# Four transformer layers on one core: stage ends and beginnings by token block, five weight slots with the low half in place

## The chip, the cores and the metric

The kernel runs on one core of one Trainium2 chip. The metric is the device time of the program in microseconds (us). Inputs and output are float32 in HBM.

## The reference

256 tokens of width 1024 pass through four layers. Layers 0 and 1 are RMS-normalised, layers 2 and 3 use LayerNorm:

```python
# layers 0, 1: MLA mixer, then dilated mixer (DIL)
h = h + rms_norm(mixer(rms_norm(h, g[0])), g[1])
h = h + rms_norm(swiglu(rms_norm(h, g[2]), ffn_w_in[i], ffn_w_out[i]), g[3])
h = h + (p[i] @ ple_w_proj[i]) * sigmoid(h @ ple_w_gate[i])
# layers 2, 3: retention, block attention and convolution side by side
h = layer_norm(alpha * h + mix(h) @ w_out)
h = layer_norm(alpha * h + (gelu(conv(h @ up_left)) * (h @ up_right)) @ w_down)
```

The hidden width of every FFN is 2816. All weights are used once, so the program is a stream of 251 weight chunks of up to 1 MB.

## The kernel before, in words

The five engines run five hand-written programs, synchronised by semaphores. The tokens form two blocks of 128 (`TB` = 2, called block 0 and block 1, `tb` in the code).

**The weight stream.** Each chunk c (128 x 2048 floats at most) takes slot c % 3. SP issues its DMA into `raw` (`stream`, line 358) once POOL has split chunk c - 3 (`lo_split`). ACT rounds it to `w_hi` (`hi_part`, line 917) once the DMA has landed and PE has used chunk c - 3 (`chunk_used`), and POOL writes the rest, `raw - w_hi`, to `w_lo` (`lo_part`, line 403). `ahead(c)` on ACT stands wherever chunk c is worked on and splits chunk c + 2. Every product is three matmuls (hi x hi, hi x lo, lo x hi; line 423).

**Two forms of product.** In a wide chunk (wo, FFN out, gate, proj, and the first chunks of layers 2 and 3) the tokens are the stationary operand and 512 columns of weights move: `wide_block` is 12 matmuls for one token block. In a tile chunk (FFN in, DIL's q and k) 128 columns of weights are stationary and the 256 tokens move: `tiles_product` is 48 matmuls for both blocks at once.

**Stage ends and beginnings.** `wide_end` takes the last two chunks of wo (of DIL, layers 2 and 3) and of FFN out for block 0, signals `y0_ready`, then takes them for block 1. DVE then makes each block's new h (`add_rms_y`, a norm by scalar Newton steps at lines 1331 and 1337, ending at line 1398; `layer_norm`, ending at line 1484), PE turns it by eight transposes (`turn_block`, line 530), ACT copies the turned tiles to `xt_hi` (lines 932 and 934), DVE writes `xt_lo` (lines 1410 and 1414), and PE begins the next stage. `begin` takes two wide chunks for block 0 and then for block 1 (gates, layers 2 and 3). An FFN or DIL begins with both blocks turned. In layers 0 and 1 the row scale of the next norm comes later: ACT squares h, DVE makes `rstd` (`rms_r`), PE spreads it (`turn_r`), and DVE multiplies the products by it.

**FFN.** Tile chunk u writes PSUM bank u % 3 of three; PE waits for `hidden_ready` of tile u - 3. DVE and ACT make the hidden tile in `conv` and `gate`. PE, ACT, POOL, SP and DVE run these stages in hardware loops (`Fori`).

**PLE.** `ple` does the gate and projection chunks whole; ACT takes both sigmoids after the last gate chunk; DVE multiplies, adds and hands h to the next stage. The split p (`p_hi`, `p_lo`) is made at the start.

## Time and profile before

| | us |
|---|---|
| median of three runs | 1620.15 (1620.07 to 1621.26) |
| the profiled execution, its own time | 1619.89 |
| its span, first to last instruction | 1618.1 |
| PE busy with matmuls | 1494.7 (92%) |
| POOL busy | 1060.0 (66%) |
| DVE busy | 840.3 (52%) |
| ACT busy | 756.2 (47%) |
| mean granted PE clock | 0.965 of full speed |

A line of the timeline reads: start, duration, engine, line of the kernel, operation, output and inputs, shape, count; in brackets the idle time of the engine before it and who ended it. Matmuls overlap in the record, so a matmul's cost is the distance between starts, not its duration. "PE psum L530 <- DVE h L1484" means that PE's instruction at line 530 waited for DVE's at line 1484.

### The profile page before, as it was taken

Reading aid. Unit: us, or ns where it says so; the run is one execution under the profiler, and the core shown is the slowest. Engines: PE = TensorE matmul, PEld = TensorE weight load, DVE = VectorE, ACT = ScalarE, POOL = GpSimd, SP = SyncE. Lnnn points to the kernel's source line nnn. Section 1 sums busy time; section 2 is a strip of 40 time slices with the busy share of each in tenths; the row PEclk is TensorE's granted clock in tenths of the full one; section 3 lists DMA queues with packets and bytes.
Section 4 is the critical chain, followed back from the end, with each engine's and each line's share of the span. In section 5 each row is a group of like instructions: output and inputs, shape, how many; then the busy total and the mean of one; then the engine's idle time right before and its main releaser. Section 6 shows DMA issues by size and latency. Waiting matters only on the chain.

```text
span 1618.1 us, 26225 instructions
## 1 busy us (share of the span) xinstructions
PE 1494.7 (92%) x10190; PEld 1372.1 (85%) x10190; DVE 840.3 (52%) x1269; ACT 756.2 (47%) x856; POOL 1060.0 (66%) x255
## 2 busy tenths in 40 slices
PE   6897999998999999989999999779999797799996
PEld 5786999878999999789987789679998697599985
DVE  5546888024222322388841254567860458568833
ACT  6774554344544444555543445235543344255531
POOL 4254788865665555568887586358888575378883
PEclk9997999999999999989999999879999899799999
DMA  5383555545555555345555555335565555245551
GB/s 208 98 293 123 182 181 182 182 156 180 174 184 162 167 171 172 130 144 181 181 182 182 183 189 182 104 105 182 181 208 182 168 172 175 78 148 183 182 214 53
DMA packets 63346, 271.15 MB, mean 168 GB/s; under 512 B 5978, under 2 KB 28688, under 8 KB 36273
## 3 DMA queue, kind: packets, MB, share of 16 engines
q1 hardware_dynamic: 38300, 242.62, 44.3%
q10 hardware_dynamic: 24981, 27.61, 5.1%
q8 instruction: 48, 0.79, 0.2%
q14 instruction: 17, 0.14, 0.0%
HBM read 269.08 MB, written 8.21 MB: 171 GB/s over the span
## 4 chain that ended last, share of the span: by engine, by line
PE 83%; DVE 11%; ACT 4%; issue 1%; POOL 1%; DMA 0%; ACTq 0%; SPq 0%; DVEq 0%
PE psum L423 81%; DVE rstd L1337 2%; DVE newton L1331 1%; PE psum L740 1%; PE psum L530 1%; ACT w_hi L917 1%; ACT xt_hi L932 1%; DVE psum L1480 1%; DVE cv L1692 1%; DVE psum L1470 1%; POOL w_lo L403 1%; DVE h L1484 1%; DVE cv L1688 0%; DVE var L1716 0%; DVE xt_lo L1410 0%
## 5 line engine op out<-in xcount | busy, mean ns | idle before, releaser
L403 POOL TENSOR_TENSOR w_lo<-raw,w_hi 128x2048 fp32r<-128x2048 f32 (+3 forms) x251 | 1059.8, 4228 | 535.5 <-ACT w_hi L917 535.2
L917 ACT ACTIVATE w_hi<-raw 128x2048 fp32r<-128x2048 f32 (+3 forms) x251 | 450.2, 1794 | 515.9 <-PE psum L423 497.0
L423 PE MATMUL psum<-xt_hi,w_hi 128*128 128x256 f32 x1984 | 569.6, 287 | 7.1 <-DVE xt_lo L1410 5.8
L423 PE MATMUL psum<-xt_hi,w_lo 128*128 128x256 f32 x1984 | 565.9, 285 | 0.0
L423 PE MATMUL psum<-xt_lo,w_hi 128*128 128x256 f32 x1984 | 565.9, 285 | 0.0
L423 PEld LDWEIGHTS psum<-xt_hi,w_hi 128*128 128x128 f32 x1984 | 385.7, 194 | 14.8 <-issue 14.7
L423 PEld LDWEIGHTS psum<-xt_lo,w_hi 128*128 128x128 f32 x1984 | 385.7, 194 | 0.1
L423 PEld LDWEIGHTS psum<-xt_hi,w_lo 128*128 128x128 f32 x1984 | 385.3, 194 | 0.0
L423 PE MATMUL psum<-w_hi,xt_hi 128*128 128x384 f32 (+3 forms) x408 | 143.3, 364 | 15.7 <-DVE xt_lo L1414 9.5
L1443 DVE TENSOR_TENSOR conv<-conv,gate 128x256 f32<-128x256 f32 x44 | 144.8, 3292 | 1.5
L423 PE MATMUL psum<-w_hi,xt_lo 128*128 128x384 f32 (+3 forms) x408 | 140.2, 357 | 0.0
L423 PE MATMUL psum<-w_lo,xt_hi 128*128 128x384 f32 (+3 forms) x408 | 140.1, 356 | 0.0
L1446 DVE CAST ht_hi<-conv 128x256 f32 x88 | 120.6, 1371 | 12.3 <-DVE conv L1443 2.1
L423 PE MATMUL psum<-w_lo,ht_hi 128*128 128x512 f32 x352 | 111.0, 396 | 0.0
L423 PE MATMUL psum<-w_hi,ht_lo 128*128 128x512 f32 x352 | 111.0, 396 | 0.0
L423 PE MATMUL psum<-w_hi,ht_hi 128*128 128x512 f32 x352 | 111.0, 396 | 0.0
L423 PEld LDWEIGHTS psum<-w_hi,xt_hi 128*128 128x128 f32 x408 | 77.8, 191 | 26.5 <-issue 11.8
L423 PEld LDWEIGHTS psum<-w_hi,xt_lo 128*128 128x128 f32 x408 | 77.9, 191 | 7.3
L423 PEld LDWEIGHTS psum<-w_lo,xt_hi 128*128 128x128 f32 x408 | 78.0, 191 | 7.0
L423 PEld LDWEIGHTS psum<-w_hi,ht_lo 128*128 128x128 f32 x352 | 66.3, 188 | 16.2
L423 PEld LDWEIGHTS psum<-w_lo,ht_hi 128*128 128x128 f32 x352 | 66.3, 188 | 16.2
L423 PEld LDWEIGHTS psum<-w_hi,ht_hi 128*128 128x128 f32 x352 | 66.0, 188 | 15.8
(214 smaller groups left out, 1484.5 us busy)
## 6 DMA issues: line engine op xcount, KB each, us to landing
raw<-w_tail SPq DMA_DIRECT2D x156, 1024.0 KB, 4.9
raw<-w_dil SPq DMA_DIRECT2D x24, 1024.0 KB, 4.8
raw<-w_mix SPq DMA_DIRECT2D x24, 1024.0 KB, 4.8
raw<-w_dil SPq DMA_DIRECT2D x16, 576.0 KB, 4.0
bias_tiles<-bias_rows ACTq DMA_DIRECT2D x1, 6912.0 KB
gbuf<-gain_rows ACTq DMA_DIRECT2D x12, 512.0 KB, 5.4
dbias<-bias_tiles ACTq DMA_DIRECT2D x16, 384.0 KB, 4.9
raw<-w_mla_a SPq DMA_DIRECT2D x3, 1024.0 KB, 7.9
```

Of the source, the lines that this page charges most:

```text
L403: nc.gpsimd.tensor_tensor(w_lo[:, s, 0:width], raw[:, s, 0:width], w_hi[:, s, 0:width].bitcast(F32), ALU.subtract).then_inc(lo_split, 1)
L423: return nc.tensor.matmul(dst, lhsT, rhs, start=start, stop=stop)
L530: ins = nc.tensor.transpose(psum[:, bank, n * P:(n + 1) * P], src[:, tb, kt * P:(kt + 1) * P], ident[:, :])
L740: ins = nc.tensor.transpose(flat[:, 5 * BANK + j * P:5 * BANK + (j + 1) * P], prob1[:, j * P:(j + 1) * P], ident[:, :])
L917: nc.scalar.activation(w_hi[:, s, 0:width], raw[:, s, 0:width], ACT.Copy).then_inc(hi_split, 1)
L932: ins = nc.scalar.activation(dst[:, kt, tok], src, ACT.Copy, scale=table_of(gains, GAINED, t, kt))
L1331: ins = v.scalar_tensor_tensor(w, y, y, half, ALU.mult, ALU.mult)
L1337: ins = v.scalar_tensor_tensor(y, w, 1.5, y, ALU.add, ALU.mult)
L1443: step(v.tensor_tensor(hid, hid, gate[:, u % SLOTS, :], ALU.mult))
L1446: step(v.tensor_copy(hi, hid))
L1470: step(v.scalar_tensor_tensor(rows, h[:, tb, :], ALPHA, rows, ALU.mult, ALU.add))
L1480: step(v.scalar_tensor_tensor(rows, rows, mv[:, tb, 0:1], gbuf[:, 0, :], ALU.subtract, ALU.mult))
```

## The change

- **Five slots, low half in place.** `raw` and `w_lo` become the same memory: POOL writes `w_lo` over `raw`. SP's DMA of chunk c waits until PE has used chunk c - 5; ACT waits only for the landing. `ahead(c)` splits chunk c + 3. ACT's copies in MLA have the true widths (1152, 512, 512 instead of 2048, 2048, 512).
- **Three last chunks by block.** `wide_end` holds three chunks: block 0 of all three, `y0_ready`, then block 1. Block 0's transposes for the next stage stand before block 1 of the last chunk (layers 0 and 1), or midway in it (layers 2 and 3). MLA and DIL end in the same way, with single blocks of wo put between the last attention steps.
- **First chunks by block.** An FFN of layers 0 and 1 and DIL begin with two tile chunks, an FFN of layers 2 and 3 with three, for block 0, then the turn of block 1, then the same chunks for block 1. `tile_part` moves 128 tokens instead of 256. Gates 2 and 3 and proj are taken by block too, with a sigmoid and an addition for each block.
- **Around it.** DVE writes `xt_lo` of block 0 before it starts block 1's norm. p is split late in each FFN, into `ot_hi` and `ot_lo`. `conv`, `gate` and `cv` share one buffer. The loops of PE, ACT, POOL and SP are written out; DVE keeps its loops.

```diff
-SLOTS = 3
+SLOTS = 5
+GROUP = 6
+LEAD = 3
+HOLD = 3
+LANES = 3
...
-        raw = sb("raw", [P, SLOTS, W])
+        with ExitStack() as part:
+            raw = sb("raw", [P, SLOTS, W], F32, part)
+        w_lo = sb("w_lo", [P, SLOTS, W], F32R)
...
-                    sp.wait_ge(lo_split, c - SLOTS + 1 + per * i)
+                    sp.wait_ge(chunk_used, c - SLOTS + 1)
...
+            def begin(t, cs, cols, part):
+                views = []
+                for k, c in enumerate(cs):
+                    views.append(chunk(c, cols))
+                    part(k, *views[k], 0)
+                turn_block(t, 1)
+                for k, view in enumerate(views):
+                    part(k, *view, 1).then_inc(chunk_used, 1)
+
+            def tile_part(t, bank0):
+                def part(k, hi, lo, tb):
+                    tok = slice(tb * P, (tb + 1) * P)
+                    for half in range(2):
+                        f = slice(half * P, (half + 1) * P)
+                        dst = psum[:, bank0 + k, half * SEQ + tb * P:half * SEQ + (tb + 1) * P]
+                        for kt in range(KT):
+                            arrive(t, tb, kt)
+                            ins = split_w(dst, hi[:, kt, f], lo[:, kt, f], xt_hi[:, kt, tok], xt_lo[:, kt, tok],
+                                          kt == 0, kt == KT - 1)
+                    return ins
+                return part
...
+            def wide_end(c, n, lhs, at, then, late, down=False, ready=lambda k: None):
+                first = n - HOLD
+                views = []
+                for k in range(HOLD):
+                    views.append(chunk(c + first + k, D))
+                    ready(k)
+                    ins = wide_block(0, first + k, *views[k], n, lhs, at, down)
                 ins.then_inc(y0_ready, 1)
+                for k, view in enumerate(views):
+                    if k == HOLD - 1 and then is not None:
+                        turn_early = lambda: turn_block(then, 0)
+                        if not late:
+                            turn_early()
+                        ins = wide_block(1, first + k, *view, n, lhs, at, down, turn_early if late else None)
+                    else:
+                        ins = wide_block(1, first + k, *view, n, lhs, at, down)
+                    ins.then_inc(chunk_used, 1)
...
+                held = 2 if l < 2 else LANES
+                begin(t, [C_IN[l] + u for u in range(held)], 2 * P, tile_part(t, FFN_AT[l]))
...
+                begin(t, (C_GATE[l], C_GATE[l] + 1), D, gate_part)
+                gates = [chunk(C_GATE[l] + m, D) for m in (2, 3)]
+                for m in (2, 3):
+                    ins = wide_block(0, m, *gates[m - 2], PROJ_N, xt, gate_at)
+                ins.then_inc(gate0_ready, 1)
+                pe.wait_ge(p_ready, l + 1)
+                proj = chunk(C_PROJ[l], D)
+                wide_block(0, 0, *proj, 1, ot, proj_at).then_inc(y0_ready, 1)
+                for m in (2, 3):
+                    wide_block(1, m, *gates[m - 2], PROJ_N, xt, gate_at).then_inc(chunk_used, 1)
+                turn_block(then, 0)
+                wide_block(1, 0, *proj, 1, ot, proj_at).then_inc(chunk_used, 1)
...
+            begin(T_DIL, (C_DIL, C_DIL + 1), 2 * P, tile_part(T_DIL, 0))
             turn_r(3, T_DIL)
+            d_tiles(2, 0)
...
-                act.wait_ge(landed[s], 16 * (c // SLOTS + 1) + 16 * turns)
-                if c >= SLOTS:
-                    act.wait_ge(chunk_used, c - SLOTS + 1 + more)
-                width = HI_WIDTHS[c]
+                act.wait_ge(landed[s], 16 * (c // SLOTS + 1))
+                width = WIDTHS[c]
...
-                if c + 2 < CHUNKS:
-                    hi_part(c + 2, more, turns)
+                if c + LEAD < CHUNKS:
+                    hi_part(c + LEAD)
...
+            def border(t, y, c, normed):
                 for tb in range(TB):
+                    if y is not None:
+                        y_squares(y, tb)
+                    if tb == 1:
+                        ahead(c)
                     turn_hi_block(t, xt_hi, tb)
+                    if normed:
+                        act.wait_ge(rows_ready, rows_of(t) + tb + 1)
+                        h_squares(tb)
```

What moves on PE at the end of FFN 0 (`ht` is the hidden tile, `h` the block to be turned, `xt` the turned h for the gates). Before, the first transposes follow the last matmul of block 1:

```order
L423 MATMUL psum<-w_hi,ht_hi 128x512 x2
L423 MATMUL psum<-w_lo,ht_hi 128x512 x2
L423 MATMUL psum<-w_hi,ht_lo 128x512 x2
L530 MATMUL psum<-ident,h 128x128 [waits rows_ready]
L530 MATMUL psum<-ident,h 128x128 x7
L423 MATMUL psum<-w_hi,xt_hi 128x512 [waits xt_ready,lo_split]
```

Now the last chunk's block 1 stands behind them:

```order
L409 MATMUL psum<-w_hi,ht_lo 128x512 x2
L535 MATMUL psum<-ident,h 128x128 [waits rows_ready]
L535 MATMUL psum<-ident,h 128x128 x7
L409 MATMUL psum<-w_hi,ht_hi 128x512 x2
L409 MATMUL psum<-w_lo,ht_hi 128x512 x2
L409 MATMUL psum<-w_hi,ht_lo 128x512 x2
L409 MATMUL psum<-w_hi,ht_hi 128x512 x2
L409 MATMUL psum<-w_lo,ht_hi 128x512 x2
L409 MATMUL psum<-w_hi,ht_lo 128x512 x2
L409 MATMUL psum<-w_hi,xt_hi 128x512 [waits xt_ready,lo_split]
```

So twelve matmuls lie between the turn of block 0 and the first gate matmul that needs it. On ACT at the same place (`gate` and `conv` are the squares' unused outputs, called `lanes` in the change), before:

```order
L944 ACTIVATE gate,stat<-psum 128x512 [waits y0_ready]
L944 ACTIVATE gate,stat<-psum 128x512 [waits y_gained]
L917 ACTIVATE w_hi<-raw 128x2048 [waits chunk_used,landed2]
L944 ACTIVATE conv,stat<-psum 128x512 [waits chunk_used]
L944 ACTIVATE conv,stat<-psum 128x512 [waits y_gained]
L934 ACTIVATE xt_hi<-psum 128x4x128 [waits turned] x4
```

and now:

```order
L960 ACTIVATE lanes,stat<-psum 128x512 [waits y0_ready]
L960 ACTIVATE lanes,stat<-psum 128x512 [waits y_gained]
L954 ACTIVATE xt_hi<-psum 128x4x128 [waits turned] x2
L960 ACTIVATE lanes,stat<-psum 128x512 [waits chunk_used]
L960 ACTIVATE lanes,stat<-psum 128x512 [waits y_gained]
L937 ACTIVATE w_hi<-raw 128x2048 [waits landed4]
L954 ACTIVATE xt_hi<-psum 128x4x128 [waits turned] x2
```

The split of the next weight chunk has moved from between the two blocks' squares to right behind block 1's, and it waits for its landing only. At the start of FFN 0 on PE, the matmuls that moved 256 tokens move 128:

```order
L409 MATMUL psum<-xt_hi,w_lo 128x128
L409 MATMUL psum<-xt_hi,w_hi 128x128
L409 MATMUL psum<-xt_lo,w_hi 128x128
L409 MATMUL psum<-xt_hi,w_lo 128x128
L535 MATMUL psum<-ident,h 128x128 [waits rows_ready]
L535 MATMUL psum<-ident,h 128x128 x7
L409 MATMUL psum<-xt_hi,w_hi 128x128 [waits xt_ready]
```

Between block 0 and block 1 of the two chunks stands only block 1's turn.

## Rows read from the trace of the kernel before

**Rows 1.** PE's waits over the whole span: total us, times, longest
```profile
PE psum L530 <- DVE h L1484: 28.9, 5, 6.2
...
PE psum L530 <- DVE h L1398: 11.7, 4, 5.5
PE psum L423 <- DVE xt_lo L1414: 10.8, 6, 3.4
PE psum L423 <- DVE xt_lo L1410: 7.9, 4, 2.5
...
PE psum L423 <- ACT probT L1091: 3.4, 3, 1.1
```

**Rows 2.** PE's timeline at the borders B0, B2, B3 and B5
```profile
129.75 1.22 PE L423 MATMUL psum<-w_hi,ot_hi 128*128 128x512 f32 x2 [2.22 <-DVE ot_lo L1573]
...
147.48 0.55 PE L423 MATMUL psum<-xt_hi,w_hi 128*128 128x256 f32 x1 [1.63 <-DVE xt_lo L1410]
...
155.95 0.60 PE L423 MATMUL psum<-ident,rstd 128*128 128x128 f32 x4
...
374.15 1.09 PE L530 MATMUL psum<-ident,h 128*128 128x128 f32 x8 [1.56 <-DVE h L1463]
...
671.62 0.66 PE L423 MATMUL psum<-ident,rinv_q 128*64 128x128 f32 x8 [1.22 <-ACT probT L1176]
...
691.77 1.97 PE L530 MATMUL psum<-ident,h 128*128 128x128 f32 x8 [5.51 <-DVE h L1398]
...
935.62 0.50 PE L423 MATMUL psum<-w_hi,xt_hi 128*128 128x512 f32 x1 [0.61 <-POOL w_lo L403]
```

**Rows 3.** PE's timeline in the first chunks: 22, 44 and 23 matmuls between starts
```profile
19.95 0.40 PE L423 MATMUL psum<-w_lo,xt_hi 128*128 128x512 f32 x1
...
24.96 0.39 PE L423 MATMUL psum<-w_hi,xt_lo 128*128 128x512 f32 x1
...
25.48 0.28 PE L423 MATMUL psum<-w_hi,xt_hi 128*128 128x160 f32 x1
...
30.40 0.28 PE L423 MATMUL psum<-w_hi,xt_lo 128*128 128x160 f32 x1
...
42.44 0.28 PE L423 MATMUL psum<-w_hi,xt_hi 128*128 128x256 f32 x1
...
45.18 0.28 PE L423 MATMUL psum<-w_hi,xt_lo 128*128 128x256 f32 x1
```

**Rows 4.** All engines, block 1 of B0: RMS norm on DVE, ACT beside it
```profile
139.06 0.68 DVE L1387 TENSOR_TENSOR t<-psum,gbuf 128x512 f32<-128x512 f32 x1
...
140.37 2.16 ACT L932 ACTIVATE xt_hi<-psum,gains 128x128 fp32r<-128x128 f32 x8
...
142.54 1.28 DVE L1398 SCALAR_TENSOR_TENSOR h<-t,rstd,h 128x1024 f32<-128x1024 f32 x1
```

**Rows 5.** DVE at the end of the program: block 0's LayerNorm begins, then block 1's
```profile
1600.32 1.23 DVE L1470 SCALAR_TENSOR_TENSOR psum<-h,psum 128x1024 f32<-128x1024 f32 x1 [48.94 <-PE psum L423]
...
1607.77 1.22 DVE L1470 SCALAR_TENSOR_TENSOR psum<-h,psum 128x1024 f32<-128x1024 f32 x1
```

**Rows 6.** All engines in block 0's LayerNorm at B7
```profile
1048.41 1.92 ACT L917 ACTIVATE w_hi<-raw 128x2048 fp32r<-128x2048 f32 x1 [6.24 <-PE psum L423]
...
1050.41 4.50 POOL L403 TENSOR_TENSOR w_lo<-raw,w_hi 128x2048 fp32r<-128x2048 f32 x1 [3.57 <-ACT w_hi L917]
1050.55 4.37 DVE L1337 SCALAR_TENSOR_TENSOR rstd<-newton,rstd 128x1 f32<-128x1 f32 x1
...
1055.21 0.16 DVE L1337 SCALAR_TENSOR_TENSOR rstd<-newton,rstd 128x1 f32<-128x1 f32 x1
```

**Rows 7.** The page's DMA issues: size, median us from issue to landing
```profile
raw<-w_tail SPq DMA_DIRECT2D x156, 1024.0 KB, 4.9
```

**Rows 8.** ACT in the third step of MLA
```profile
80.64 1.92 ACT L917 ACTIVATE w_hi<-raw 128x2048 fp32r<-128x2048 f32 x1
...
88.05 0.62 ACT L917 ACTIVATE w_hi<-raw 128x512 fp32r<-128x512 f32 x1
```

More of the change, by code:

```diff
@@ L895, in _ @@
                 t = (T_RET2, T_RET3)[n]
-                turn(t, t1, block_ready(t))
+                for tb in range(TB):
+                    turn_block(t, tb, t1)
                 pe.wait_ge(cv_copied, 3 * n + 3)
@@ L960, in turn_hi_rms, with squares, h_squares, y_squares @@
-            def turn_hi_rms(t):
-                for tb in range(TB):
+            def squares(tb, src, col, n=D, at=0):
+                return nc.scalar.activation(unused[tb][:, at:at + src.shape[-1]], src, ACT.Square, scale=n ** -0.5,
+                                            accum_out=stat[:, col:col + 1])
+            def h_squares(tb):
+                squares(tb, h[:, tb, :], 2 * TB + tb).then_inc(h_squared, 1)
+            def y_squares(y, tb):
+                if tb == 0:
+                    act.wait_ge(y0_ready, YS.index(y) + 1)
+                else:
+                    act.wait_ge(chunk_used, y_chunk(*y) + 1)
+                rows = y_rows(y, tb)
+                squares(tb, rows[:, 0:BANK], 2 * tb).then_inc(squared, 1)
+                act.wait_ge(y_gained, TB * RMS_YS.index(y) + tb + 1)
+                squares(tb, rows[:, BANK:], 2 * tb + 1, at=BANK).then_inc(squared, 1)
@@ L1042, in _, with mla_heads @@
                                      accum_out=stat[:, TB + tb:TB + tb + 1]).then_inc(squared, 1)
-            turn_hi(T_MLA_C, xt_hi)
+            for tb in range(TB):
+                turn_hi_block(T_MLA_C, xt_hi, tb)
             gq, gk = MLA_GROUP * MLA_HD, MLA_GROUP * NOPE
-            def mla_heads(at, more=0, turns=0, between=None, after=None):
+            def mla_heads(at, between=None, after=None):
                 c = C_MLA + 3 * at
-                ahead(c, more, turns)
+                ahead(c)
                 if between is not None:
                     between()
-                act.wait_ge(chunk_used, c + 1 + more)
+                act.wait_ge(chunk_used, c + 1)
                 for tb in range(TB):
@@ L1070, in mla_heads @@
                     after()
-                ahead(c + 1, more, turns)
+                ahead(c + 1)
             def mla_qT(step):
@@ L1597, in _ @@
             add_rms_y(("out", 0), 1, 1, T_PLE0)
[L1598 to L1601 removed]
+            ple(0, T_DIL)
             rms_r()
```

521 lines of the change are left out of this document (221 added, 300 removed).

## The prediction

> **What bounds the kernel now.** I read the waits of TensorE (PE) first, then PE's timeline at the ends of the stages, then what the vector engine (DVE), the scalar engine (ACT) and POOL do there. Inside the FFN and DIL stages PE has no gap; its gaps lie where one stage hands a normalised h to the next. [Rows 1] sum them: 28.9 and 11.7 us for h of a token block, 10.8 and 7.9 for the low half xt_lo of the turned h, DVE the releaser every time. [Rows 2] show single ones. After a long gap PE runs at its lower clock (1.2 instead of 2.4 GHz): the 48 matmuls of the first chunk of FFN 0 lie between 147.48 and 155.95, 8.5 us, where they take 5.7 at full clock, and eight transposes at 691.77 take 1.97 instead of the 1.09 at 374.15. Call the borders B0 (wo to FFN 0), B1 and B4 (FFN to the gate of layers 0 and 1), B2 (layer 0 to DIL), B3 (to FFN 1), B5 (layer 1 to layer 2), B7 and B10 (wo to FFN 2 and 3), B8 (layer 2 to 3), and the end.
>
> **The price of working by token block.** From [rows 3], starts divided by the matmuls between them: 160 columns 4.92/44 = 0.112 us, 256 columns 2.74/23 = 0.119, 512 columns 5.01/22 = 0.228. From 256 to 512 columns the step is about 0.107 us, so the moving data go at 0.42 ns a column; at that slope 160 columns should take 0.079. They take 0.112: a floor that isn't the moving data. Weights (w) of 128 columns stand in front of every one of these matmuls, and I take this floor for 128 columns too. The bounds are 0.066 (the slope alone) and 0.112. The value is the upper one, since 160 is the nearest row and already lies on the floor. The Trainium skill (TensorE: Matmul & The Clock Gate, on LDWEIGHTS) gives the load of a weight as its columns over 1.2, 107 ns for 128: by that rule the row agrees. The same page's sustained roofline says about 81 ns a matmul at N=128, which would make the extra 24.7 us instead of 59.8; it stands beside rival (b).
>
> The wide chunks (wo, out, gate, proj, mix) hold the tokens as weights and move 512 columns of w, so they split by block for nothing: 12 matmuls, 2.7 us a block. A tile chunk (FFN in, DIL) moves the tokens. Split, its 48 matmuls of 256 columns become 96 of 128: 96 x 0.1115 = 10.7 us for 48 x 0.119 = 5.7, **5.0 us more a chunk**. Two chunks at B0, B2, B3 and three at B7, B10 are 12 chunks: **+59.8 us** of PE time that was not there.
>
> **What the tile borders give back.** Before, gaps and half clock [rows 1, 2], the slow matmuls estimated as in the first chunk of FFN 0: B0 2.2+2.2+3.3+1.6 and some 5.5 slow, 14.8; B2 1.6+2.5 and 1.7 slow, 5.8; B3 5.5+1.6, two waits of 1.2 in the last DIL pair and 3.2 slow, 12.8; B7 12.1 (6.2, 5.2 and 0.7; it and B10 hold 22.8 of the 28.9) and about 4.3 slow, 16.4, B10 the same. Together 66.2.
> New gaps: PE now has 10.7 or 16 us of work on block 0 while DVE makes block 1's h, but still waits for its own transposes: 1.9 us each time where gains are applied in four steps (half the transposes, ACT's four steps of 0.29, DVE's the same), 1.0 elsewhere. B0 2 x 1.9; B2 1.9, and 1.4 because the third chunk takes the first one's bank and so waits for turn_r, rb_dil and the first dqk (before, a chunk lay between); B3 2 x 1.9 plus 1.4 (exponentials of the last pair behind only one 2.7 us block) and 1.9 (o_scaled, ot_hi, ot_lo with nothing between values_sum and wo's last chunk); B7 and B10 0.6 and 1.0. Together 17.4. Net of the five borders: 59.8 - 66.2 + 17.4 = **+11.0 us**.
>
> **The other borders.** One norm takes DVE 4.8 us in RMS form [rows 4] and 7.45 in LayerNorm form [rows 5].
> B1 and B4: block 0 is ready 0.3 us after PE asks, Z (the last chunk) then covers its turn, and the gates' block 0 gives 5.4 us of cover to block 1's norm of 4.8. That would be 1.2 us better than before. But ACT's order puts the split of the next chunk right behind the second square of block 1. In [rows 4] ACT's next instruction begins 1.31 us after DVE's first (T), a split takes 1.92 and POOL follows 0.08 later, at T+3.31; h begins at T+3.48. [Rows 6] show what then happens: POOL begins 0.1 us before an rstd that takes 0.16 elsewhere, and the rstd takes 4.37, to the end of POOL's 4.50. So I take h1 at T+9.1 instead of T+4.8; PE waits 3.7 us, turns and begins block 1 at half clock: **+5 us each**, bounds -1.2 and +7. The Trainium skill (SBUF — State Buffer, on the shared port pair) has it that a DVE operation with two SBUF inputs and a GpSimd one that reads SBUF exclude each other for a whole instruction; the rows agree. At B0 and B3 the same collision comes, but the 10.7 us of block 0 hide it.
> B5: **-2.2** (a gap of 2.3 goes, of the 10.8, and the wait of 0.6 for w_lo [rows 2]; 1.0 comes). B8: before 6.1+3.4+0.2 of gaps and 2.9 slow; now 0.3 for block 0, 2.9 for block 1 (7.45 plus 0.9 behind POOL, against 5.5 of cover), 0.9 for the turn and 1.5 slow: **-7.0**. The end: three blocks instead of two lie between y0_ready and the last matmul, 8.4 us, longer than block 0's 7.45, so block 1's norm begins right at the last matmul instead of 2.0 us later: **-2.0**.
>
> **The rest.** The slots: a chunk's DMA now starts when the chunk five before is used; it takes 4.9 us [rows 7], the split 1.9, POOL 4.5, 11.4 together against four chunks of 5.5 or more. No wait, if that holds. MLA: ACT splits 512 columns where it split 2048, 0.6 for 1.9 us [rows 8], ahead of probT, in two of the three steps where PE waits 3.4 us in all for it [rows 1]: **-2.2** (0 to -3.4). Start: the third split now precedes the squares; the Newton steps move 2 us into POOL's three operations: **+1.5** (0 to +3). PE's loops written out: FFN's matmuls are 0.001 us apart wider than straight ones, 72 chunks: **-2** (0 to -4.7). The p split moves to ACT and DVE inside FFN, where both wait for PE: 0; if not, a DVE operation of 0.7 us ahead of a border.
>
> **Sum.** 11.0 + 10 - 2.2 - 7.0 - 2.0 - 2.2 + 1.5 - 2 = +7.1. The profiled execution's time is 1619.9 (span 1618.1; 0.3 below the median of 1620.15): the profiled one would come to 1627.0, and the difference to the median lies inside every other uncertainty here: **1627**.
>
> **Rivals.**
> (a) POOL comes late at B1 and B4: the margin is 0.17 us. If POOL begins 0.2 us later than I reckon, h goes first. 2 x 6.2 less: 1614.6, **faster**. For it: both ends move with every semaphore; against: in [rows 6] POOL was in just that place. Chance 0.2.
> (b) 128 columns cost less than the floor of 160, because the next weights load partly behind the matmul: say 0.085 us, between the bounds. Then 1152 x 0.0265 = 30 less, some 8 of it returned as waits for h1 at B0 and B3: 1605. Against it are the matmuls of 160 columns, same types, 48 in a row. Chance 0.05. With the skill's 81 ns (the page above) it would be 35 less instead of 30.
> (c) The covers are worth more than I count: all gaps of more than 2 us go, the clock stays up, and my new gaps (17.4 us, each by handovers of 0.05 to 0.1) are a third too large, 5.8 less: 1621, no change. Chance 0.22.
> (d) Refill too late: SP's request waits for PE and no longer for POOL, and near the borders three chunks are held. If a landing takes 10 us there, two waits of 2 to 4 us come at each of four borders: +15, 1640. Against it: 4.9 us at 1 MB, and five slots. Chance 0.06.
> My forecast has 0.47.
>
> **The numbers.** A measurement of this kernel tells from no change what is over 0.2%, 3.2 us. Slower: forecast 0.47 less its lower edge, and (d): 0.5. Same: (c) and part of the forecast's edge: 0.22. Faster: (a), (b) and the low side of (c): 0.28. The range reaches from 1608, inside (a) with its bounds, to 1635, B1 and B4 at +7 with start and MLA at their worse ends; the forecast's own is 1620 to 1634.
>
> **What would show it.** Matmuls xt,w of 128 columns: 1152, starts 0.11 us apart. At B1 and B4 an h of 5 to 6 us instead of 1.3 with POOL beside it. B7's gaps gone but the stretch from Z to the fourth chunk no shorter. DVE's last operation 2 us nearer to PE's last. I am wrong if the 128-column matmuls lie under 0.09 us apart, if h at B1 takes 1.3 us, or if PE waits for POOL's w_lo inside stages.

## The result, and the profile after

The changed kernel takes **1732.05 us** (median of 4 runs, 1727.69 to 1733.49), the one before 1620.33 in the same session: ratio **1.0684, 95% interval 1.0663 to 1.0705**. The forecast was 1627, range 1608 to 1635. The direction was right and the size was not: 7 us more were expected, and 112 came. The direction is not owed to the causes that were missed: with both of them removed (below) the changed kernel still takes 1639.46. The profiled execution took 1730.88, with a span of 1729.1.

PE is busy for 93% of the span, so the lost time is not in long gaps. The waits of PE over the whole span, total, times, longest (against [rows 1]):

```profile
PE psum L409 <- DVE ht_lo L1458: 31.4, 26, 1.7
PE psum L535 <- DVE t L1729: 17.5, 2, 8.8
PE psum L409 <- DVE xt_lo L1421: 10.9, 6, 2.0
PE psum L535 <- DVE h L1409: 8.2, 3, 3.6
...
PE psum L409 <- DVE xt_lo L1425: 6.9, 6, 1.5
PE psum L857 <- ACT mvr L1272: 4.8, 2, 2.6
PE psum L535 <- DVE h L1497: 4.3, 4, 2.8
```

What the change was made for happened: the waits for h of a LayerNorm fell from 28.9 to 4.3 us. But at the top is a wait that [rows 1] do not have: for ht_lo, the last thing that DVE makes of an FFN tile. Busy time by stretch, for PE, PEld (PE's weight loads), DVE, ACT and POOL, with the number of instructions, then the granted clock of TensorE (1.00 is full), the share and the GB/s of the DMA; first the kernel after, then the one before:

```profile
150.00:200.00 50.00, 46.96 (x272) 46.36 (x272) 27.23 (x46) 15.39 (x21) 19.49 (x5) 0.66 0.29 95
200.00:250.00 50.00, 46.02 (x378) 45.21 (x377) 44.22 (x40) 17.50 (x15) 36.46 (x9) 1.00 0.48 163
...
426.00:446.00 20.00, 20.00 (x97) 20.00 (x97) 7.71 (x23) 3.53 (x5) 7.03 (x3) 0.51 0.33 92
...
1154.00:1189.00 35.00, 34.02 (x303) 33.78 (x302) 18.41 (x30) 11.00 (x10) 17.43 (x4) 1.00 0.28 92
1550.00:1600.00 50.00, 50.00 (x419) 50.00 (x418) 40.60 (x53) 20.70 (x18) 40.67 (x9) 1.00 0.53 181
```
```profile
150.00:200.00 50.00, 50.00 (x406) 50.00 (x406) 39.55 (x46) 26.40 (x23) 38.05 (x9) 0.97 0.45 152
200.00:250.00 50.00, 50.00 (x419) 50.00 (x419) 41.57 (x42) 27.61 (x23) 40.53 (x9) 1.00 0.53 184
```

There are two separate losses. At the starts of FFN 0 (150 to 200), DIL (426 to 446) and FFN 1 PE is busy nearly all the time at a clock of 0.51 to 0.66 (FFN 1: 0.56 from 750 to 800). And inside FFN 0, at full clock, PE does 378 matmuls in 50 us instead of 419, and POOL is busy for 36.46 us instead of 40.53. FFN 3, at 1550, is as fast as before.

**The clock.** PE at the start of FFN 0, in DIL's second block, after it at the end of FFN 0's split, and at FFN 2 (start, duration):

```profile
138.91 0.28 PE L409 MATMUL psum<-xt_hi,w_hi 128*128 128x128 f32 x1
...
139.36 0.28 PE L409 MATMUL psum<-xt_lo,w_hi 128*128 128x128 f32 x1
139.47 0.37 PE L409 MATMUL psum<-xt_hi,w_lo 128*128 128x128 f32 x1
139.64 0.41 PE L409 MATMUL psum<-xt_hi,w_hi 128*128 128x128 f32 x1
```
```profile
425.73 0.33 PE L409 MATMUL psum<-xt_hi,w_hi 128*128 128x128 f32 x1 [1.95 <-DVE xt_lo L1421]
...
426.43 0.42 PE L409 MATMUL psum<-xt_hi,w_lo 128*128 128x128 f32 x1
426.64 0.41 PE L409 MATMUL psum<-xt_hi,w_hi 128*128 128x128 f32 x1
```
```profile
183.59 0.41 PE L409 MATMUL psum<-xt_hi,w_lo 128*128 128x256 f32 x1
183.80 0.32 PE L409 MATMUL psum<-xt_hi,w_hi 128*128 128x256 f32 x1
183.96 0.28 PE L409 MATMUL psum<-xt_lo,w_hi 128*128 128x256 f32 x1
```
```profile
1154.22 0.28 PE L409 MATMUL psum<-xt_lo,w_hi 128*128 128x128 f32 x1
1154.33 0.27 PE L409 MATMUL psum<-xt_hi,w_lo 128*128 128x128 f32 x1
```

The starts lie 0.11 us apart at first, as forecast. Then, 1.3 us into running matmuls at 139.47 and 0.5 us into them at 426.23, the distance becomes 0.213: half clock (1.2 GHz). In both places PE had waited 2.0 us for xt_lo just before. (A wait of that length does not always do it: in the run with the products in PSUM, below, the first block of FFN 0 ran at 0.112 throughout behind a wait of 2.05 us, and the second, behind 1.96, at 0.214.) The distance stays there for 84 and 95 matmuls at FFN 0, 90 in DIL, 85 and 95 at FFN 1, and rises at 183.80, 1.4 us after the first 256-column matmuls. At FFN 2 and 3, where the waits ahead of the two blocks are 0.6 (for h) and 1.0 us (for xt_lo), all 288 keep 0.112. In the kernel before, where 256-column matmuls began at 147.48 [rows 2], the granted clock was full again at 153.5. The Trainium skill (TensorE: Matmul & The Clock Gate, The HAM clock gate) has it that the slow state is the default "and activity releases the throttle". The rows of DIL do not agree: PE is busy for 20.00 of 20.00 us at a granted clock of 0.51, and the measurement decides. The 449 slow matmuls (84 + 95 + 90 + 85 + 95) at 0.101 us more each are **45 us**.

**The FFN tile.** DVE in FFN 0, one tile and the cast of the next; then POOL, of which the first row is two operations; then ACT:

```profile
238.61 3.55 DVE L1454 TENSOR_TENSOR lanes<-lanes 128x256 f32<-128x256 f32 x1
242.29 4.48 DVE L1457 CAST ht_hi<-lanes 128x256 f32 x1
246.90 0.43 DVE L1458 TENSOR_TENSOR ht_lo<-lanes,ht_hi 128x256 f32 x1
...
249.17 0.29 DVE L1457 CAST ht_hi<-lanes 128x256 f32 x1
```
```profile
237.25 9.38 POOL L401 TENSOR_TENSOR w_lo<-raw,w_hi 128x2048 fp32r<-128x2048 f32 x2 [3.37 <-ACT w_hi L937]
249.99 4.63 POOL L401 TENSOR_TENSOR w_lo<-raw,w_hi 128x2048 fp32r<-128x2048 f32 x1 [3.37 <-ACT w_hi L937]
```
```profile
247.69 0.42 ACT L1001 ACTIVATE lanes<-lanes 128x256 f32<-128x256 f32 x1 [7.27 <-DVE lanes L1438]
248.01 1.90 ACT L937 ACTIVATE w_hi<-raw 128x2048 fp32r<-128x2048 f32 x1
```

Before the change (DVE, then POOL, FFN 0):

```profile
206.07 3.49 DVE L1443 TENSOR_TENSOR conv<-conv,gate 128x256 f32<-128x256 f32 x1
209.70 0.29 DVE L1446 CAST ht_hi<-conv 128x256 f32 x1
210.12 0.43 DVE L1447 TENSOR_TENSOR ht_lo<-conv,ht_hi 128x256 f32 x1
```
```profile
204.65 4.62 POOL L403 TENSOR_TENSOR w_lo<-raw,w_hi 128x2048 fp32r<-128x2048 f32 x1 [1.13 <-ACT w_hi L917]
210.41 4.62 POOL L403 TENSOR_TENSOR w_lo<-raw,w_hi 128x2048 fp32r<-128x2048 f32 x1 [1.14 <-ACT w_hi L917]
```

Before, in FFN 0 and 1, each tile met one POOL operation: DVE's multiply waited for its end at 209.27, and cast and subtraction just fitted into the 1.14 us in which POOL rested. After, POOL does two chunks one behind the other (9.38 us); the multiply waits for the first (3.55) and the cast for the second (4.48). ACT's gate stands 7.27 us behind DVE, its next split behind the gate, and POOL then idles 3.37 us with two chunks to come. This cycle of two tiles takes 9.38 + 3.37 = 12.75 us, where PE needs 11.5, and it repeats: PE's waits for ht_lo come 12.8 us apart, 9 each in FFN 0 and 1, and 8 in FFN 2, there 13.5 apart. The 256-column matmuls of the hidden stages: 960 each in 127.8 us in FFN 0 and 1, 912 in 124.0 in FFN 2 and in 109.6 in FFN 3. At FFN 3's 0.1201 us 960 take 115.3, so the loss is 12.5 + 12.5 + 14.4 = **39 us**. One collision a tile costs PE nothing: in FFN 2 and 3 of the kernel before, every cast is held by POOL already (2.0 to 2.9 us where 0.29 is needed), and PE has no wait for ht_lo; FFN 3 after the change is the same (1.8 to 3.7 us).

**What the forecast had right** stands in the same trace. The collision at B1 (DVE, then POOL):

```profile
377.58 0.16 DVE L1353 SCALAR_TENSOR_TENSOR rstd<-newton,rstd 128x1 f32<-128x1 f32 x1
377.77 5.46 DVE L1409 SCALAR_TENSOR_TENSOR h<-t,rstd,h 128x1024 f32<-128x1024 f32 x1
```
```profile
377.58 4.57 POOL L401 TENSOR_TENSOR w_lo<-raw,w_hi 128x2048 fp32r<-128x2048 f32 x1 [9.71 <-ACT w_hi L937]
```

POOL began 0.19 us ahead of h (reckoned: 0.17), h took 5.46 instead of 1.3, and PE waited 3.56 (reckoned: 3.7).

### The profile page after: what moved, and what is told of

Read it like the earlier page. It is cut to its first block, busy times and chain, and to the rows that moved or that the text cites. A ratio compares the mean times of both kernels' runs of the same rounds, so it can differ in the third digit from the quotient of the medians.

```text
span 1729.1 us, 25398 instructions
## 1 busy us (share of the span) xinstructions
PE 1610.5 (93%) x10766; PEld 1481.2 (86%) x10766; DVE 927.6 (54%) x1270; ACT 674.8 (39%) x805; POOL 1061.8 (61%) x255
## 4 chain that ended last, share of the span: by engine, by line
PE 65%; DVE 25%; ACT 4%; issue 4%; DMA 1%; DVEq 1%; SPq 0%; ACTq 0%
PE psum L409 62%; DVE ht_hi L1457 7%; DVE lanes L1454 4%; ACT lanes L1001 1%; PE psum L535 1%; DVE newton L1347 1%; PE psum L751 1%; DVE lanes L1453 1%; DVE lanes L1438 1%; DVE h L1409 1%; ACT xt_hi L952 1%; DVE lanes L1699 1%; DMA raw<-w_mix 1%; DVE lanes L1445 1%; DVE lanes L1446 1%
## 5 line engine op out<-in xcount | busy, mean ns | idle before, releaser
L409 PE MATMUL psum<-xt_hi,w_hi 128*128 128x256 f32 (+1 forms) x2176 | 641.1, 295 | 43.7 <-DVE ht_lo L1458 31.4
L409 PE MATMUL psum<-xt_lo,w_hi 128*128 128x256 f32 (+1 forms) x2176 | 635.3, 292 | 0.0
L409 PE MATMUL psum<-xt_hi,w_lo 128*128 128x256 f32 (+1 forms) x2176 | 635.3, 292 | 0.0
L409 PEld LDWEIGHTS psum<-xt_hi,w_hi 128*128 128x128 f32 x2176 | 440.1, 202 | 57.5 <-DVE ht_lo L1458 36.6
L409 PEld LDWEIGHTS psum<-xt_hi,w_lo 128*128 128x128 f32 x2176 | 440.4, 202 | 0.0
L409 PEld LDWEIGHTS psum<-xt_lo,w_hi 128*128 128x128 f32 x2176 | 440.3, 202 | 0.1
L1457 DVE CAST ht_hi<-lanes 128x256 f32 x88 | 195.3, 2219 | 12.3 <-DVE lanes L1454 2.1
L1001 ACT ACTIVATE lanes<-lanes 128x256 f32<-128x256 f32 x88 | 36.8, 418 | 309.6 <-DVE lanes L1438 192.0
L409 PE MATMUL psum<-w_hi,ht_lo 128*128 128x512 f32 x352 | 111.0, 396 | 0.0
L409 PE MATMUL psum<-w_lo,ht_hi 128*128 128x512 f32 x352 | 111.0, 396 | 0.0
L1458 DVE TENSOR_TENSOR ht_lo<-lanes,ht_hi 128x256 f32 x88 | 88.0, 1000 | 10.5
L1454 DVE TENSOR_TENSOR lanes<-lanes 128x256 f32<-128x256 f32 x44 | 88.4, 2009 | 1.5
```

The lines of the kernel that those rows point to most:

```text
L409: return nc.tensor.matmul(dst, lhsT, rhs, start=start, stop=stop)
L1001: nc.scalar.activation(gate[:, u % LANES, :], conv[:, u % LANES, :], func).then_inc(gate_ready, 1)
L1454: step(v.tensor_tensor(hid, hid, gate[:, u % LANES, :], ALU.mult))
L1457: step(v.tensor_copy(hi, hid))
L1458: v.tensor_tensor(lo, hid, hi.bitcast(F32), ALU.subtract).then_inc(hidden_ready, 1)
```

## The experiments

Eighteen kernels ran in five sessions, each beside the kernel before (1620.35 to 1622.17). Ratios are to it.

### The two losses apart

**Gate first.** In ACT's FFN loop the two lines change places.

```diff
-                    ahead(C_IN[l] + u + 1)
                     act.wait_ge(conv_ready, l * FT + u + 1)
                     nc.scalar.activation(gate[...], conv[...], func)...
+                    ahead(C_IN[l] + u + 1)
```

> In ACT's FFN loop the gate activation of tile u stands before the split of the chunk ahead instead of behind it. Theory L (POOL's start against DVE's operations): the split then begins after the gate, some 1.0 us after PE's chunk ends, and POOL some 3.0 us after it, when DVE has finished the tile; each tile meets POOL at most once. The waits of PE for ht_lo (31.4 us in FFN 0, 1 and 2) go, and with them the longer output stages: 12.4 + 12.6 + 14.4 + 4.9, about 44 us less, 1688. Theory A (only ACT's gate is late, because it stands behind a split that waits for its DMA) expects the same time, but with POOL's operations still falling on DVE's cast or multiply about as often. Theory M (the matmul program written out, or five slots, makes PE itself slower) expects no change, 1732.

Measured: 1711.03 (1.0583, 1.0536 to 1.0629). The waits went in FFN 2 (hidden stage 158.2 to 143.8) and stayed in FFN 0 and 1 (18 of them, 16.9 us), 12.7 to 12.8 us apart. Only part of theory L's forecast came: the order on ACT alone does not break the cycle.

**Half of POOL's work.**

```diff
+                if any(C_IN[l] <= c < C_OUT[l] + FFN_OUT_N for l in range(4)):
+                    width //= 2
                 nc.gpsimd.tensor_tensor(w_lo[:, s, 0:width], ...)
...
+                    part = w_lo[:, s, 0:n * cols // 2].rearrange("p (k n) -> p k n", n=cols)
...
+                            return part[at[0], at[1] % (n // 2), at[2]]
```

> Leaves out half of POOL's subtraction for the chunks of the FFNs (1024 of 2048 columns; PE takes the finished half twice). Order on ACT unchanged. Theory L: a POOL operation of 2.3 us instead of 4.6 cannot hold DVE for a tile's time, PE waits for ht_lo fall to under 2 us, time 1688. Theory A: ACT's gate stays late by the same amount, PE's waits stay at 25 to 31 us, time 1725 to 1732. Theory M: 1732.

Measured: 1686.66 (1.0366, 1.0304 to 1.0428), and no wait of PE for ht_lo is left. Theories A and M fall: ACT's order was untouched.

**Products in PSUM.**

```diff
+                    hid = bank[:, SEQ:2 * SEQ]
                     if l < 2:
                         step(v.tensor_tensor(hid, bank[:, SEQ:2 * SEQ], rb_ffn[:, :], ALU.mult))
```

> DVE's products of the FFN tile stay in PSUM (multiply, cast and subtraction then read at most one operand from SBUF) instead of in the SBUF lanes; nothing else changes. Theory L (POOL's operation and a DVE operation on SBUF operands exclude each other): multiply, cast and subtraction no longer wait for POOL and take 0.3 to 0.5 us each, PE's waits for ht_lo go, 44 to 46 us less, 1687, like the run with half of POOL's work. If the lock takes in every cast and every SBUF operand, also with PSUM on one side, the mean of the three stays over 1 us and the time near 1732.

Measured: 1686.84 (1.0404, 1.0386 to 1.0421), the waits gone. POOL (first row) and DVE side by side:

```profile
253.77 4.62 POOL L401 TENSOR_TENSOR w_lo<-raw,w_hi 128x2048 fp32r<-128x2048 f32 x1 [1.20 <-ACT w_hi L937]
```
```profile
254.50 0.43 DVE L1455 TENSOR_TENSOR psum<-psum,lanes 128x256 f32<-128x256 f32 x1
255.07 0.42 DVE L1458 CAST ht_hi<-psum 128x256 f32 x1
255.62 0.42 DVE L1459 TENSOR_TENSOR ht_lo<-psum,ht_hi 128x256 f32 x1
```

All run inside POOL's 4.62 us. So the collision is between POOL's operation and DVE operations whose operands lie in SBUF. The Trainium skill (SBUF — State Buffer, on the shared port pair) has the rule: a DVE operation in a 2-port mode, or one with two SBUF inputs against a GpSimd operation that reads SBUF, shuts out the GpSimd one or is shut out by it for a whole instruction, whoever starts first. The rows agree, the cast included: 0.29 alone and blocked from SBUF, 0.42 and never blocked from PSUM.

**POOL's work in halves.**

```diff
-                nc.gpsimd.tensor_tensor(w_lo[:, s, 0:width], ...).then_inc(lo_split, 1)
+                for part in (slice(0, width // 2), slice(width // 2, width)):
+                    ins = nc.gpsimd.tensor_tensor(w_lo[:, s, part], ...)
+                ins.then_inc(lo_split, 1)
```

> The changed kernel with POOL's subtraction of a chunk as two operations of 1024 columns instead of one of 2048 (the same work, 2 x 2.35 us). If DVE loses by the length of one operation (a waiting DVE operation comes in at each boundary): in the cycle of two tiles DVE's multiply, cast and subtraction each wait 2.3 us at most, a tile is done 2 us sooner, the waits for ht_lo go, h of block 1 at the borders from FFN to gate takes 3.2 instead of 5.5: 44 + 4 less, 1684. If it loses by POOL's whole work (POOL takes its next operation before DVE gets in): 1728 to 1732. If each of DVE's operations now meets an operation of POOL's (up to 3 x 2.3 a tile instead of one of 3.5): over 1740.

Measured: 1679.90 (1.0341, 1.0310 to 1.0371). PE's waits for ht_lo are 3.0 us in all. The first row is POOL's, four operations:

```profile
199.18 9.91 POOL L402 TENSOR_TENSOR w_lo<-raw,w_hi 128x1024 fp32r<-128x1024 f32 x4 [2.95 <-ACT w_hi L939]
```
```profile
202.01 2.28 DVE L1459 CAST ht_hi<-lanes 128x256 f32 x1
204.41 2.41 DVE L1460 TENSOR_TENSOR ht_lo<-lanes,ht_hi 128x256 f32 x1
```

DVE comes in at each boundary. The total of POOL's work is unchanged; the length of one operation was the price.

**The gaps filled.** Two fp32 matmuls of 512 columns, never read, in each wait for xt_lo at FFN 0, DIL and FFN 1.

```diff
+            def fill(bank, tb):
+                for _ in range(2):
+                    mm(psum[:, bank, :], ident[:, :], h[:, tb, 0:BANK], True, True)
...
+                if t in (T_FFN0, T_FFN1):
+                    fill({T_FFN0: 1, T_FFN1: 7}[t], 0)
...
                 turn_block(t, 1)
+                if t in (T_FFN0, T_DIL, T_FFN1):
+                    fill({T_FFN0: 0, T_DIL: 4, T_FFN1: 1}[t], 1)
```

> Two fp32 matmuls of 512 columns (result never read, 0.85 us each at full clock) are put into PE's wait for its own transposes at FFN 0 (both blocks), DIL (second block) and FFN 1 (both). Theory C1: the clock falls because of the idle 2 us before, and 128-column matmuls do not bring it back up; without the gap some 450 matmuls go at 0.112 instead of 0.213 us, 45 us less, 1687. Theory C2: a stream of 128-column matmuls with gains loses the clock by itself, gap or no gap: 1732 to 1736, granted clock at 150 to 200 us still 0.66.

Measured: 1678.19 (1.0351, 1.0334 to 1.0368), 54 less. PE at FFN 0's second block, and the clock:

```profile
146.35 1.88 PE L409 MATMUL psum<-h,ident 128*128 128x512 f32 x4
148.47 0.33 PE L409 MATMUL psum<-xt_hi,w_hi 128*128 128x128 f32 x1 [0.24 <-DVE xt_lo L1429]
148.63 0.28 PE L409 MATMUL psum<-xt_lo,w_hi 128*128 128x128 f32 x1
148.75 0.28 PE L409 MATMUL psum<-xt_hi,w_lo 128*128 128x128 f32 x1
```
```profile
135.00:160.00 25.00, 24.17 (x204) 22.72 (x202) 21.45 (x41) 11.64 (x20) 13.37 (x3) 1.00 0.23 79
```

The same 128-column matmuls keep full clock if the gap before them is filled (0.3 us of it are left): C1, not C2. The waits for ht_lo were now in FFN 0, 1 and 3 (156.2 us) and not in FFN 2: which LayerNorm layer falls into the cycle changes from kernel to kernel.

**The fill too late.** Six of these matmuls behind the wait instead of in it.

```diff
                 turn_block(t, 1)
+                if t in (T_FFN0, T_DIL, T_FFN1):
+                    for kt in (0, 4):
+                        arrive(t, 1, kt)
+                    for _ in range(6):
+                        mm(psum[:, {T_FFN0: 0, T_DIL: 4, T_FFN1: 1}[t], :], ident[:, :], h[:, 1, 0:BANK], True, True)
```

> Changed kernel with six fp32 matmuls of 512 columns (never read) behind the wait for the second block's transposes, not in it, at FFN 0, DIL and FFN 1; the gap itself stays. Theory C1 (128-column matmuls do not raise a clock that fell; denser ones do): the clock is back at full after a few of the six, and stays there through the 96 matmuls of 128 columns: 3 x 96 x 0.101 = 29 less, the six cost 5.1 us at full and 10.2 at half clock, 3 x 7 = 21: 1724, with second blocks at a pitch of 0.112. If the 128-column matmuls lose the clock again by themselves: pitch 0.213 in most of them, 1732 + 25 = 1757.

Measured: a median of 1725.17, but with 1703.4 to 1734.89 between runs no ratio is given. The trace answers the question. The clock before and after the six at FFN 0:

```profile
140.00:157.00 17.00, 17.00 (x81) 17.00 (x81) 7.16 (x11) 1.80 (x2) 4.55 (x1) 0.50 0.00 0
169.00:180.00 11.00, 11.00 (x99) 10.76 (x98) 3.58 (x4) 0.00 (x0) 3.21 (x1) 1.00 0.28 95
```

The clock is back at full behind the six, and it stays there through the 95 matmuls that follow, at FFN 0, DIL and FFN 1 alike; the first block of FFN 0, which has the gap and no such matmuls, is slow in 82 of 95 as before. So the same work runs at either clock, by what stands ahead of it. (The cycle came in FFN 0 and 1, and in parts of FFN 2 and 3, so the time is not that of the clock alone.)

**Whole first chunks at FFN 0, DIL, FFN 1.**

```diff
+                if t in (T_FFN0, T_DIL, T_FFN1):
+                    turn_block(t, 1)
+                    for k, c in enumerate(cs):
...
+                        tiles_product(c, (FFN_AT[0] if t == T_FFN0 else 0 if t == T_DIL else FFN_AT[1]) + k)
+                    return
```

> At FFN 0, DIL and FFN 1 both blocks are turned first and the first two tile chunks run whole, on 256 columns; at FFN 2 and 3 the split stays. Under C1: the clock falls in the longer gap (7 us) but 256-column matmuls raise it again in a few us, as before the change. The six split chunks cost 121.7 us now (43.5 + 34.0 + 43.7 and the gaps between their blocks inside them); whole they cost 6 x 5.7 = 34 and some 10 us of half clock, and 7 + 5 + 7 us of gaps for the second block: 121 - 34 - 10 - 19 = 58 us less, 1674. If whole chunks stay at half clock too (C3: something else in the change holds the clock down), 6 x 10.3 = 62: about 28 less, 1704.

Measured: 1681.29 (1.0373, 1.0355 to 1.0390); 1674 was expected under C1, 1704 under C3. FFN 0's hidden stage took 141.6, with 8 waits for ht_lo in it. The missing 7: h of a block took 5.41 us beside POOL here too, and PE waited 11.78 for h of block 1 at FFN 0 and at FFN 1, where the estimate had 7.

**Both remedies.** The filled gaps and the products in PSUM.

> Both remedies together: the filled gaps and the products in PSUM. If the clock and the lock are independent causes, the time is that of the fill (1678) less all its waits for ht_lo (26.8) and their tail in the output stages (about 2): 1650. If they overlap, 1665 to 1680.

Measured: **1639.46** (1.0115, 1.0098 to 1.0132), no wait for ht_lo at all. 93 of the 112 us are these two causes; where the rest lies is in the table of "Why the prediction was wrong".

### How the cycle starts

**rstd between the second-block parts.** The layer's rstd, transposed by `turn_r`, is what DVE's first FFN operation needs.

```diff
                 for k, view in enumerate(views):
                     part(k, *view, 1).then_inc(chunk_used, 1)
+                    if k == 0 and t in (T_FFN0, T_FFN1):
+                        turn_r({T_FFN0: 2, T_FFN1: 4}[t], t)
```

> On top of the run with the filled gaps (1678): in FFN 0 and 1 the transposed rstd is made between the two second-block parts, not behind both. Theory B (both held tiles become DVE's at the same moment, and this backlog of two throws DVE and POOL into a cycle of two tiles in 12.8 us instead of 11.5, from which they don't come out): tile 0 is now done before tile 1 exists, so the waits for ht_lo in FFN 0 and 1 go, 2 x 13 less, and PE waits 7 us in each for rstd, which POOL's two splits hold up: 1666. If the cycle comes anyway (it is the steady state, whatever the start), only the 2 x 7 are added: 1692.

Measured: 1695.60 (1.0474, 1.0440 to 1.0508; single runs 1685.0 to 1705.0), on the base of 1678. PE waited 6.6 us for rstd in each layer, as said. Behind that wait the 48 matmuls of the second part ran at a distance of 0.214 in both layers, half clock again, 9.5 us together that neither theory had. In FFN 0 the waits for ht_lo went, all of them; in FFN 1 six stayed, and FFN 2 had nine. So a backlog can start the cycle, but without it the cycle comes too.

**The split tied to PE again.**

```diff
+                    act.wait_ge(chunk_used, C_IN[l] + u + 1)
                     ahead(C_IN[l] + u + 1)
```

> On top of the run with the filled gaps (1678): in the FFNs ACT's split of the chunk ahead also waits for PE to have used tile u, so POOL's start hangs on PE's end of a chunk again, as before the change, and no longer on the landing. Theory D (what let POOL slip against DVE is that the split follows the DMA): the waits for ht_lo go in all FFNs, 1651. Theory B (a backlog of tiles at the stage's start and ACT's order, split behind gate, keep the cycle of two tiles alive): FFN 0 and 1 keep their waits (24 us), since there the split already stands behind a late gate: 1675 to 1680.

Measured: 1656.02 (1.0234, 1.0193 to 1.0275), 22 less than its base. FFN 2 and 3 are both at 143.8 and FFN 1 at 144.8; FFN 0 keeps 9 waits of 10.8 us together (156.6). Mostly theory D, with B's remainder in FFN 0.

**The backlog put into the kernel before.**

```diff
                 pair(0, 0, t)
+                pair(1, 0)
                 if l < 2:
                     turn_r((2, 4)[l], t)
-                for u in range(1, SLOTS):
+                for u in range(2, SLOTS):
```

> The kernel before with rstd transposed behind the second FFN chunk instead of the first (layers 0 and 1), so that DVE gets two tiles at once. Theory B1 (two tiles at once are enough for the cycle): waits for ht_lo in FFN 0 and 1, 13 each, 1647. Theory B2 (it also takes the five slots, which let ACT and POOL do two chunks one behind the other; with three slots a split has to wait for PE, so that POOL cannot hold DVE twice): no change, 1621 to 1624.

Measured: 1628.75 (1.0041, 1.0025 to 1.0056): 2 waits for ht_lo, 4.2 us, and no cycle; behind each wait the granted clock was 0.72 (178 to 184 and 729 to 735), some 1.7 us more each time. That is B2, though 5 us over its number. The reason that it gives: with three slots ACT may only split a chunk when PE has used one, so POOL does not get two in a row in mid-stage. With the run before, this points to the five slots with a split that follows the landing as what lets the cycle live; as a part on its own it was not put into the kernel before, so this stays argued in part.

### Versions meant to beat both

**n1**: all first tile chunks whole, fills, products in PSUM, and ACT's split at the borders behind the turn.

```diff
-                    if tb == 1:
-                        ahead(c)
                     turn_hi_block(t, xt_hi, tb)
+                    if tb == 1:
+                        ahead(c)
```

> A version meant to beat both: the changed kernel with the FFN products in PSUM, all first tile chunks whole (256 columns; rstd transposed behind the first), unread fp32 matmuls in the remaining gaps before them, and at the borders ACT's split of the next chunk behind the second block's turn instead of behind its squares, so that POOL does not stand beside h. From 1639.5: FFN 0, 1: 14.6 of extra time and gaps become 7.8, DIL 12.3 become 5, FFN 2, 3: 16.6 become 8.5 each, and 4 each at the two borders from FFN to gate: 13.6 + 7 + 16 + 8 = 45 less, 1595. If the fills do not hold the clock there: 10 to 15 more, 1608.

Measured: 1638.03 (1.0104, 1.0088 to 1.0121). The moved split brought POOL beside the Newton steps; PE waited 20.5 us in 3 times for rstd, 9.5 the longest, and twice 4.4 us for POOL's w_lo in the gates of layers 0 and 1, where the kernel after has no such wait. POOL did three chunks in a row from 716.20 to 729.76; DVE beside it:

```profile
720.79 4.55 DVE L1362 SCALAR_TENSOR_TENSOR newton<-rstd,nhalf 128x1 f32<-128x1 f32 x1
725.37 4.48 DVE L1368 SCALAR_TENSOR_TENSOR rstd<-newton,rstd 128x1 f32<-128x1 f32 x2
```

**n2**: the kernel before, with fills in PE's gaps ahead of FFN 0 to 3 and DIL (3 to 8 ahead of the first turn, 2 to 6 between the turns, 1 or 3 behind).

```diff
+                    for _ in range(n):
+                        mm(psum[:, bank, 0:3 * P], ident[:, :], mask[:, 0:3 * P], True, True)
```

> The kernel before with unread fp32 matmuls of 384 columns in PE's gaps ahead of FFN 0 to 3 and DIL, and nothing else. If half clock after a gap costs what its rows show (5.5 at FFN 0, 1.7 at DIL, 3.2 at FFN 1, 4.3 each at FFN 2 and 3, and the slow transposes), and the fills never outlast the wait: about 18 less, 1603. Where a fill outlasts the wait, up to 5 of it come back: 1608.

Measured: 1622.12 (1.0003, 0.9994 to 1.0012). The slow matmuls went, and nothing was gained in sum. At FFN 0 PE then waited 1.99 us for rstd and began the second chunk at 156.33, where it had been at 156.31: half clock in a stretch that rstd bounds cost nothing there. In DIL it did harm. PE was done with its chunk sooner, so ACT split the next one sooner, POOL did two in a row (7.29 us, from 381.01) beside the Newton steps, and two of DVE's small operations were held instead of one; PE waited 4.41 us for rstd, and the way from FFN 0's output to DIL's second pair took 136.2 us instead of 131.0. At FFN 2 and 3, which have no such rstd, the stretches became 1.7 and 0.3 us shorter, not the 4.3 each of the estimate.

**n3**: fill and PSUM products, first chunks of FFN 2 and 3 whole with fills, POOL in halves (the edits shown above, the whole chunks with `t in (T_FFN2, T_FFN3)`).

> From the run with fill and PSUM products (1639.5): the first chunks of FFN 2 and 3 whole with fills in the gaps (in the run with whole chunks these two borders and hidden stages together came 13 us shorter), and POOL's operations halved: h and rstd wait less, 2 x 2 at the borders from FFN to gate, little elsewhere. 1639.5 - 13 - 4 = 1622. If halves make new collisions, 1626 to 1632.

Measured: 1622.40 (1.0007, 0.9997 to 1.0017): level with the kernel before, as forecast.

**n4, n5**: the kernel before with the edit of POOL's halves, and with n2's fills as well.

> The kernel before with POOL's operations halved, nothing else. If the length of one operation is what the waits for h and rstd at its borders contain (4.4 us where 0.16 is needed, at FFN 2 and 3, some 2 elsewhere): 2 x 2.2 + 2 x 1 less, 1616. In its FFNs DVE's one blocked operation of 3.5 us becomes two of up to 2.3: if the last of the three then misses the 1.1 us in which POOL rests, PE waits appear: over 1625.

> The kernel before with the fills of the earlier run (1622, in which PE waited 8.4 us for rstd instead of running slow matmuls) and POOL's operations halved. If the wait for rstd is POOL's length: 8.4 becomes 3 to 4, and the rest as in the run with halves alone: 1611. If not: 1618 to 1622.

Measured: 1620.55 (1.0000, 0.9989 to 1.0010) and 1622.01 (1.0006, 0.9997 to 1.0015). No change in either; in n5 PE still waits 7.8 us for rstd, as two DVE operations of the chain each wait for one half.

**n6, n7**: n1 without its move on ACT, with POOL in halves and with five fills instead of three ahead of FFN 0 and 1 (n6), and the same with `range(0)` in the fills (n7).

> All first tile chunks whole, fills in the gaps, products in PSUM, POOL's operations halved. Against the level version (1622.4): FFN 0 and 1 lose 10.0 us of extra matmul time and 4.6 of gaps each, and get the second block's h (some 6.5 with one half of POOL's operation beside it), its turn (0.9), gains (2.3) and some 2 for rstd: 14.6 - 11.7 = 3 each; DIL 12.3 become 9: 3. 1613. If splitting pays there after all (waits for rstd of 7 us and more, as in the earlier whole version): 1625 or more.

> The same without the fills. Slow matmuls of 256 columns after five gaps, 3 to 5 us each by the kernel before's rows, where nothing else is late behind them: 12 to 18 more than with fills, 1628. If, as in the kernel before, the next wait (rstd, or DVE's first tile) swallows them: within 4 us of it.

Measured: 1627.05 (1.0036, 1.0025 to 1.0046) and 1631.50 (1.0064, 1.0050 to 1.0078). Against n3, whole chunks at FFN 0, DIL and FFN 1 cost 4.7 us. At FFN 0 and 1 waits for h (5.3 us each) and for rstd (9.2 us together, against 2.6) stand in the split's place, and the stretches to their outputs are 4.1 and 5.7 us longer than n3's. At DIL the whole form is the better one: the way to its second pair is 2.9 us shorter (135.9 against 138.8). So with nothing else in the way splitting pays at FFN 0 and 1 and not at DIL; a version split in just this way was not run. No version beats the kernel before.

## Why the prediction was wrong, and where it was right

The run with both remedies meets the two conditions under which the sum was made. Its stages, from the traces, against the forecast (us; the first column is the kernel before's own length; milestones are PE's first matmul of a stage):

| stretch | before | after | both remedies | forecast |
|---|---|---|---|---|
| start to FFN 0's output | 277.3 | +32.7 | -2.2 | -1.7 |
| to DIL's second pair (B1, B2) | 131.0 | +25.9 | +12.6 | +12.5 |
| to FFN 1's output (B3) | 416.5 | +37.8 | +6.0 | +4.3 |
| to FFN 2's output (B4, B5, B7) | 371.0 | +20.0 | +5.6 | +3.0 |
| to FFN 3's output (B8, B10) | 348.0 | -3.6 | -3.6 | -6.8 |
| to the end | 74.2 | -1.8 | -1.8 | -2.0 |
| sum | 1618.1 | +111.0 | +16.6 | +9.3 (+7.1 with the loops' -2 and rounding) |

- **"Split, its 48 matmuls of 256 columns become 96 of 128 ... 5.0 us more"**: right, 0.112 us at full clock in all 1152 in the run with both remedies, where no wait ahead of them is over 1.0 us. Rival (b) is refuted.
- **"New gaps ... 1.9 us each time"**: the gaps came as said (10.9 us in 6 waits). The step that failed is that they were priced as idle time alone. The clock fell behind them and did not rise among 128-column matmuls: 45 us. The prediction had counted half clock in the old gaps by rows with 256 columns and, but for 1.5 us at B8 and a part of B1 and B4, carried none over to the new ones.
- **"No wait, if that holds"** (the slots), and with it "FFN's matmuls" at -2: failed. The refill did hold, POOL's w_lo was on time inside the stages. But the reckoning asked only whether a chunk is ready for PE, not when POOL's operation falls against DVE's. In FFN 0 and 1 of the trace of before, cast and subtraction had 1.14 us between two POOL operations and took 0.85: that was to be seen, and I did not price it. 39 us and some in the output stages.
- **B1 and B4, POOL beside h**: right in mechanism and size (h takes 5.46 us, PE waits 3.56 at B1 and again at B4). Rival (a) is refuted; with a margin of 0.19 us this was a near thing, as the prediction had said.
- **B8 and the end**: right. In the trace of after, block 1's h at B8 lets PE wait 2.81 us (reckoned: 2.9) and its turn 0.98 (0.9). With both remedies the way from FFN 2's output to layer 3's first tile chunk is 6.8 us shorter (reckoned: 7.0). The 5.8 us by which the fourth and fifth stretch miss the forecast lie for the most part inside the mixers, in a wait that I had not seen: PE waits 4.8 us for mvr (a copy out of PSUM that ACT makes there) after the change, 2.0 before. ACT in the mixer of layer 3:

```profile
1441.84 1.91 ACT L937 ACTIVATE w_hi<-raw 128x2048 fp32r<-128x2048 f32 x1 [1.52 <-DMA raw<-w_mix]
1443.66 0.79 ACT L1272 ACTIVATE mvr<-psum 128x768 f32<-128x768 f32 x1
```

  The copy stands behind splits that now wait for their DMA. That is rival (d), the late refill, at a place and a size (1.4 us a layer) that it did not name. With both remedies the wait is 5.5 us, 3.5 more than before, and behind it the 36 small matmuls of layer 3's mixer run at a granted clock of 0.72 (1348 to 1354), 1.4 us more: 4.9 of the 5.8 us. It is the step that failed for the gaps once more, at another place.
- None of the rivals was what came. My signs of error named a wait for POOL's w_lo inside the stages; it was one for DVE's ht_lo.

Not settled: what decides in which LayerNorm layer the cycle starts (FFN 2 in some kernels, FFN 3 in one, a part of both in one, neither in others), why FFN 0 keeps it when the split is tied to PE again, and whether the loops written out gave their 2 us, which was not tried alone.

## What to carry to other kernels

A stage that is "hidden" may hold because two engines happen to take turns: where one operation of 4.6 us shuts out another engine's, look at the time left between two of them, and shorten the operation or move the operands to PSUM before changing what starts it. A gap costs what the work behind it costs at half clock until the clock rises, so ask what kind of matmuls follow it. And price a gap or slow matmuls in the old kernel only after asking which wait would stand there without them: here filling them gained nothing, and at one place a PE that was sooner done only brought POOL back beside DVE sooner.
